# Three transformer layers on one core: bias added on the vector engine, lone matmuls at nine groups, a finer start and two interleaved output blocks

## The reference

```python
# first block: x = x + rms(mixer_a(rms(x))); x = x + (p @ w_pp) * sigmoid(x @ w_pg)
q, k, v, g = split(h @ w_in_a, 4)                # 16 heads of 128
z = q k^T * scale; later = reverse cumulative sum of log_sigmoid(-z), strictly causal
o = exp(log_sigmoid(z) + later) v;  out = (o * silu(g)) @ w_out_a
# second block: the same frame, mixer_b: latent attention
ckv, k_rope = rms(x) @ w_dkv; cq, g = rms(x) @ w_in_b
o = softmax((q_nope k_nope + q_rope k_rope) * scale, chunk mask) v
# third block
q, k, v, gate_b, gate_c, hc = split(rms(x) @ w_in_2)
logits = q1 k1 + rel_bias[bucket(i - j)], the same for q2 k2;   # 8 heads, halves of 64 rows
a = (softmax1 - lam * softmax2) v, rms-normed by head
c = rms(gate_b * causal_conv3(gate_c * hc))
x = x + rms(concat(a, c) @ w_out_2)
x = x + rms((silu(rms(x) @ w_gate) * (rms(x) @ w_up)) @ w_down)   # width 5632
```

## Time and profile before

| | us |
|---|---|
| median of 3 runs (lowest, highest) | 2254.36 (2251.59, 2256.01) |
| the profiled execution | 2259.11 |
| its span, first to last instruction | 2257.3 |
| PE busy | 2207.5 |
| DVE, ACT busy | 1382.3, 1156.2 |

### The profile page before, as it was taken

One profiled execution on the slowest core, in us unless ns is written; L12 is line 12 of the kernel. 1 busy time (PEld: TensorE's weight loads), 2 busy tenths in 40 slices (PEclk: granted clock), 3 DMA queues, 4 the chain that ended last, 5 costly groups with the idle time before them and its releaser, 6 DMA issues.

```text
span 2257.3 us, 29264 instructions
## 1 busy us (share of the span) xinstructions
PE 2207.5 (98%) x12060; PEld 1884.6 (83%) x12060; DVE 1382.3 (61%) x1740; ACT 1156.2 (51%) x1510; POOL 8.9 (0%) x20
## 2 busy tenths in 40 slices
PE   7999999999999999999999999989999999999997
PEld 6888888888878888888887888878888888888886
DVE  6555545557777565577657686567556544565644
ACT  5455454555665555566544443556444444444543
POOL 0000000000000000000000000000000000000000
PEclk9999999999999999999999999999999999999999
DMA  6555555465556445565654545645656666666654
GB/s 218 170 166 162 185 163 181 145 193 187 180 159 182 136 128 162 177 187 178 197 166 142 157 150 163 190 142 177 193 180 196 192 194 193 188 186 196 202 179 151
DMA packets 228677, 394.57 MB, mean 175 GB/s; under 512 B 24921, under 2 KB 50146, under 8 KB 228416
## 3 DMA queue, kind: packets, MB, share of 16 engines
q1 hardware_dynamic: 227312, 389.40, 56.3%
q0 software_dynamic: 800, 2.45, 0.4%
q10 hardware_dynamic: 432, 0.85, 0.1%
HBM read 390.55 MB, written 2.11 MB: 174 GB/s over the span
## 4 chain that ended last, share of the span: by engine, by line
PE 77%; DVE 11%; DMA 6%; ACT 4%; issue 1%; SPq 0%; DVEq 0%; ACTq 0%
PE ps L790 77%; DVE WL L1253 4%; DMA RAW<-in_w_ple_gate 2%; ACT WH L1015 1%; DVE TMP L1253 1%; DVE xT L1253 1%; PE ps L794 1%; DMA RAW<-in_w_out_a 1%; DMA RAW<-in_w_out 1%; ACT T L1015 1%; ACT SQ L1015 1%; DVE T L1253 1%; DMA RAW<-in_w_dkv 1%; DVE ACC L1253 0%; DVE H L1256 0%
## 5 line engine op out<-in xcount | busy, mean ns | idle before, releaser
L1253 DVE TENSOR_TENSOR WL<-RAW,WH 128x1024 fp32r<-128x1024 f32 x734 | 890.1, 1222 | 495.7 <-ACT WH L1015 492.1
L1015 ACT ACTIVATE WH<-RAW 128x1024 fp32r<-128x1024 f32 x734 | 773.1, 1058 | 761.5 <-PE ps L790 316.1
L790 PE MATMUL ps<-H,WH 128*128 128x512 f32 x3152 | 1123.8, 400 | 10.1 <-DVE H L1256 4.8
L790 PE MATMUL ps<-H,WL 128*128 128x256 f32 x3152 | 884.8, 281 | 0.0
L790 PEld LDWEIGHTS ps<-H,WH 128*128 128x128 f32 x3152 | 593.8, 188 | 152.6 <-issue 5.7
L790 PEld LDWEIGHTS ps<-H,WL 128*128 128x128 f32 x3152 | 597.5, 190 | 1.3
L790 PE MATMUL ps<-O,WH 128*128 128x512 f32 x1344 | 477.7, 400 | 7.8 <-DVE WL L1253 3.2
L790 PE MATMUL ps<-O,WL 128*128 128x256 f32 x1344 | 376.1, 280 | 0.0
L790 PEld LDWEIGHTS ps<-O,WH 128*128 128x128 f32 x1344 | 252.7, 188 | 72.6 <-DVE WL L1253 6.3
L790 PEld LDWEIGHTS ps<-O,WL 128*128 128x128 f32 x1344 | 253.9, 189 | 0.3
L790 PE MATMUL ps<-WH,ACTS 128*128 128x512 f32 x704 | 218.3, 390 | 0.0
(11 more groups left out here) (206 smaller groups left out, 1381.2 us busy)
## 6 DMA issues: line engine op xcount, KB each, us to landing
RAW<-in_w_in_a SPq DMA_DIRECT2D x128, 512.0 KB, 4.0
RAW<-in_w_in SPq DMA_DIRECT2D x96, 512.0 KB, 3.9
RAW<-in_w_gate SPq DMA_DIRECT2D x88, 512.0 KB, 4.4
RAW<-in_w_up SPq DMA_DIRECT2D x88, 512.0 KB, 4.5
RAW<-in_w_down SPq DMA_DIRECT2D x88, 512.0 KB, 4.8
RAW<-in_w_ple_gate SPq DMA_DIRECT2D x64, 512.0 KB, 4.5
RAW<-in_w_in_b SPq DMA_DIRECT2D x40, 512.0 KB, 3.8
RAW<-in_w_out_a SPq DMA_DIRECT2D x32, 512.0 KB, 4.1
```

Source lines behind the costliest of these rows:

```text
L790: return e.matmul(o, l, r, start=start, stop=True, skip_group_check=True)
L1015: return e.activation(o, i, f, **kw)
L1253: return e.tensor_tensor(o, x, y, op)
```

## The change

- **Start.** x comes in five pieces (256, 256 and three of 512 KB); the first two chunks hold one k each; pieces 4 and 5 are loaded behind the first `split_lo` steps; the x copies from the third on are ACT's; constants and masks are issued by POOL once the last x piece is in, ahead of its own small loads.
- **Bias.** `c_scores` drops the flips. q is stored with its positions backwards in each half, `c_bias`, a new step, adds RT to the scores in PSUM on DVE, and the product is read backwards by ACT, which takes over the copy and the square. A head's task is two half-chunks longer.
- **Lone matmuls.** A group with `lead` begins with one, in its own bank: block 1 of each output projection, pg0 and pg2 of both blocks, fg1 and fg6.
- **Order.** Taps of `cfir` are steps of their own; the products of the last convolution block are foreground steps; its ones matmul goes to bank 7, so that no two banks of the ring are skipped; the third projection has blocks of 4, 2, 4, 4, 2, its first two fed by turns for the first eight k; masks come first in `a_cum` and `b_scores`; ACT's copy of the latent is a step after DVE's; pp2 and pp3 exchange their second banks.

```diff
+OUTB2 = ((0, 4), (4, 2), (6, 4), (10, 4), (14, 2))
+XPARTS = ((0, 2), (2, 4), (4, 8), (8, 12), (12, 16))
...
-        ci = len(g.chunks) * g.per
-        ks = g.kts[ci:ci + g.per]
+        ci = g.fed
+        ks = g.kts[ci:ci + (1 if ci < g.ones else g.per)]
+        g.fed += len(ks)
...
+        def backwards(ap):
+            dims = [list(d) for d in ap.ap]
+            step, n = dims[-1]
+            return bass.AP(ap.tensor, ap.offset + step * (n - 1), dims[:-1] + [[-step, n]])
...
+                    elif n_ == 0:
+                        pl.begin(g)
+                        pl.begin(gs[1])
+                        for _ in range(2):
+                            pl.feed(g)
+                            pl.feed(g)
+                            pl.feed(gs[1])
+                    if norm == "mixpost" and n_ < 2:
+                        pl.rest(g)
...
-                pl.evict(pp(2, late[0:2]))
+                pl.evict(pp(2, late[0::3]))
                 units[2]()
-                pl.evict(pp(3, late[2:4]))
+                pl.evict(pp(3, late[1:3]))
...
-                units += [both(do("lat_norm", name, 0), do("lat_norm", name, 2)), low[0], low[1]]
+                units += [both(do("lat_norm", name, 0), do("lat_norm", name, 2)),
+                          both(do("lat_high", name, 0), do("lat_high", name, 2)), low[0], low[1]]
...
-                    do("c_scores", hd, bank=[6, 7]), do("c_soft", hd), None, do("c_prob", hd), None, None,
+                    do("c_scores", hd, bank=[6, 7]), do("c_bias", hd), do("c_soft", hd), None, do("c_prob", hd), None, None, None,
...
-                pl.fg.append(task(do("cfir", m, 0), do("cfir", m, 1, makes=[("cfir", m, 1)])))
+                pl.fg.append(task(do("cfir", m, 0, 0), do("cfir", m, 0, 1), both(do("cfir", m, 0, 2), do("cfir", m, 1, 0)),
+                                  do("cfir", m, 1, 1), do("cfir", m, 1, 2, makes=[("cfir", m, 1)])))
...
-                else:
-                    pl.put("conv", m, 0)
-                    pl.put("conv", m, 1)
             pl.h2_read = pl.last_chunk()
-            b = pl.take(2)[0]
-            pl.fg.append(task(None, both(*rstd("conv", b=b)),
+            pl.fg.append(task(do("conv", 1, 0), do("conv", 1, 1, makes=[("conv", 1, 1)]), both(*rstd("conv", b=7)),
...
+                    if first and g.lead and j == 0 and t == 0:
+                        mm(ps[:, b, 0:S], C["ones"], C["cos"], True)
...
-                        mm(ps[:, b, 0:P], q[:, 0:P], k[:, 0:P], True)
-                        mm(ps[:, b, P:384], q[:, P:S], k)
-                        mm(ps[:, b, 0:P], C["flip"], RT[:, hd, P:S])
-                        m = mm(ps[:, b, P:384], C["flip"], RT[:, hd, :])
+                        mm(ps[:, b, 0:P], q[:, P:S], k[:, 0:P], True)
+                        m = mm(ps[:, b, P:384], q[:, 0:P], k)
...
+                elif kind == "c_pv":
+                    pv_ = backwards(halves(ps[:, 6, 0:S]))
+                    ac.wait_ge(at("pv", "C", hd))
+                    act(halves(F2[:, 0, 0:S]), pv_, ACT.Square).then_inc(*ev(act_att, ("csq", hd)))
+                    act(halves(F2[:, 1, 0:S]), pv_, ACT.Copy).then_inc(*ev(act_att, ("ccopy", hd)))
...
+                elif kind == "c_bias":
+                    dv.wait_ge(at("scores", "C", hd), at("in", "rt"))
+                    tt(ps[:, 6:8, 0:P], ps[:, 6:8, 0:P], bc(RT[:, hd, P:S]), ALU.add)
+                    tt(ps[:, 6:8, P:384], ps[:, 6:8, P:384], bc(RT[:, hd, :]), ALU.add).then_inc(*ev(dve_att))
```

More of the change, by code:

```diff
@@ L107 @@
     one: bool = False
+    back: bool = False
+    lead: bool = False
     slow: bool = False
     late: bool = False
+    ones: int = 0
     k0: int = 0
     war: tuple = ()
+    fed: int = 0
     banks: list = field(default_factory=list)
@@ L209, in rest @@
     def rest(self, g):
-        while len(g.chunks) * g.per < len(g.kts):
+        while g.fed < len(g.kts):
             self.feed(g)
@@ L334, in bc, with halves, goal, blocks_of @@
             return ap.unsqueeze(1).broadcast_to([P, n, ap.shape[-1]])
+        def backwards(ap):
+            dims = [list(d) for d in ap.ap]
+            step, n = dims[-1]
+            return bass.AP(ap.tensor, ap.offset + step * (n - 1), dims[:-1] + [[-step, n]])
+        def halves(ap):
+            return ap.rearrange("p (b n) -> p b n", b=2)
+        def goal(g, p):
+            if g.tmp:
+                return TMPG[g.tmp0 + p][:, :, :]
+            dst = g.dst[:, 2 * p:2 * p + g.width(p), :]
+            return backwards(dst) if g.back else dst
+        def blocks_of(norm):
+            return OUTB2 if norm == "mixpost" else OUTB
         def tiles(t, c):
@@ L391, in ordered @@
             xgain(0)()
+            pl.splits(1)
+            xgain(2)()
             xfetch(4)()
-            xgain(2)()
             units = [both(xfetch(c + 2), xgain(c)) if c + 2 < KD else xgain(c) for c in range(4, KD, 2)]
@@ L433, in ordered @@
                 norm = "pre0" if j else ""
-                head(f"q{j}", 512 * j, qT[s], war, scale=P ** -0.5, norm=norm, late=not j)
+                head(f"q{j}", 512 * j, qT[s], war, scale=P ** -0.5, norm=norm, late=not j,
+                     ones=0 if j else 2)
                 head(f"k{j}", D + 512 * j, kT[s], war, norm=norm, late=not j)
@@ L766, in sq_source @@
                 out_ = {"post0": "out0_", "post1": "out1_", "mixpost": "out2_"}[norm]
-                return tiles(T, 2 * i), ("sum", f"{out_}{i // 2}", i % 2) if i < 6 else ("sum", f"{out_}{i - 3}", 0)
+                n_, t0 = next((n_, t0) for n_, (t0, nt) in enumerate(blocks_of(norm)) if t0 <= 2 * i < t0 + nt)
+                return tiles(T, 2 * i), ("sum", f"{out_}{n_}", i - t0 // 2)
             if norm == "kv":
@@ L866, in tensor_engine @@
                     b = 4 + c // 2 % 2
-                    pe.wait_ge(at("in", f"x{c // 4}"), at(*war) if war else None)
+                    part = next(m for m, (c0, c1) in enumerate(XPARTS) if c0 <= c < c1)
+                    pe.wait_ge(at("in", f"x{part}"), at(*war) if war else None)
                     for j in range(2):
@@ L886, in tensor_engine @@
                         mm(ps[:, b, 0:S], C["ones"], SQ[:, 1, :]).then_inc(*ev(summed_sq, ("ones", norm)))
-                elif kind == "lone":
-                    pe.wait_ge(at(*args[0]))
-                    mm(ps[:, 7, 0:S], C["ones"], C["cos"], True).then_inc(*ev(summed_sq, ("lone",)))
                 elif kind == "rcols":
@@ L1066, in scalar_engine @@
                     m.then_inc(*ev(copied, ("free", g.name, 0), ("ready", g.name, 0)))
+                elif kind == "xfetch" and args[0] >= 4:
+                    c = args[0]
+                    ac.wait_ge(at("xt", c))
+                    act(tiles(xT, c), ps[:, 4 + c // 2 % 2, :].rearrange("p (j s) -> p j s", j=2), ACT.Copy).then_inc(
+                        *ev(x_high, ("xcopy", c)))
                 elif kind == "xgain":
@@ L1672, in sync_engine, with load_x @@
             e.dma_start(CS[:, 0:P], cst[:, 0:P]).then_inc(*ev(landed["ident"], ("in", "ident"), by=16))
[L1673 to L1674 removed]
+            def load_x(m):
+                c0, c1 = XPARTS[m]
+                e.dma_start(XN[:, :, P * c0:P * c1], xr[:, :, P * c0:P * c1]).then_inc(
                     *ev(landed[f"x{m}"], ("in", f"x{m}"), by=16))
[L1676 to L1677 removed]
+            for m in range(NRAW):
+                load_x(m)
+                load_chunk(m)
             for kind, *args in steps:
```

102 lines of the change are left out of this document (47 added, 55 removed).

## The result

The changed kernel takes **2224.48 us** (median of four runs, 2222.07 to 2226.67) where the kernel before takes 2254.33. The ratio is 0.9869 with a 95% interval of 0.9853 to 0.9884, so 29.9 us less. Measured again later, beside other kernels, the ratio was 0.9874 (0.9854 to 0.9893). Forecast: 2226 us.

The account below looks back on a forecast made before the run. TensorE was taken to bound the kernel. Start -6.0, bias -13.6, stalls -5.0, lone matmuls -3.2 and the rest -0.5 sum to -28.3 us: 2230.8 us for the profiled execution, 2226 us for the median, range 2215 to 2240.

Parts of the forecast that it names:

- What bounds the kernel: Whole kernel: TensorE, busy 2207.5 of 2257.3 us; gains only by less work, closer spacing, or less of its 50 idle us.
- Part 1: Start: x in pieces, one-k chunks, later constants bring the first dense matmul from 15.74 to 9.3 us; -6.0 us.
- no new wait: Start: chunks 3 and 4 are requested while earlier pairs still lie ahead of TensorE, so no added wait was expected.
- The slow beginning: Start: the first seven pairs, 4.65 us at the 1.2 GHz level, were taken to move along unchanged with the earlier start.
- Part 2: Third block's head scores: without flips, two q-by-k blocks take 1.6 us instead of 3.3; -13.6 us for eight heads.
- rival A: Head scores: the two 64-row blocks overlap, saving 0.65 us more per head, 5.2 us more; 2221 us; chance 0.12.
- Part 3: Convolution and third projection: reordering answers stalls of 1.51, 1.10, 0.40, 0.38 and 2.36 us, sum 5.75; -5.0 us.
- no stall above 0.5 us: Sign to check: TensorE has no longer stall between 1140 and 1400 us of the new span.
- Part 4: Eight more lone matmuls at group starts cost 3.4 us and buy 6.6 through 6.3 ns closer pair spacing; -3.2 us.
- Rival B: Convolution stalls only move and close spacing does not last: -0.5 and +2 instead of -8.2; 2236 us; chance 0.22.
- C: Start gains nothing, as ACT with the x copies becomes the bound or the slow level lasts longer; 2232 us; chance 0.06.
- D: Third block's heads: DVE, adding the bias in PSUM, becomes the bound and takes back the gain; 2256 us; chance 0.03.

Follow-up runs that it names:

- experiment 12: Changed kernel with the old start: x in four pieces, whole chunks, x copies on DVE, constants and masks from ACT's queue at once; 2229.01 us, ratio 0.9877.
- experiment 1: Changed kernel with the two 64-row score blocks of each third-block head half a chunk apart, dense pairs between them; 2231.46 us, ratio 0.9879.
- experiment 2: Changed kernel with the second block's scores reordered: masks, then both 64-row rope products side by side, then the 128-row products; 2218.21 us, ratio 0.9820.
- experiment 4: Kernel before, flips kept, with the third block's two 64-row score products side by side, then the two flips; 2250.69 us, ratio 0.9961.
- experiment 7: Changed kernel with the convolution and the third projection's block order as they were before; 2232.12 us, ratio 0.9891.
- experiment 6: Changed kernel without the eight new lone matmuls, the one at fg6 kept; 2227.80 us, ratio 0.9877.
- experiment 3: Changed kernel with no weight split put ahead of the first group's last chunk, so q0's eviction comes before the next split; 2222.68 us, ratio 0.9840.
- experiment 11: Changed kernel with rope products side by side, q0's eviction ahead of split and square, lone matmul at fg2 instead of fg1, none at fg6; 2221.10 us, ratio 0.9851.
- experiment 8: Changed kernel with the second block's rope products side by side and q0's eviction ahead of the next split and square; 2216.72 us, ratio 0.9826.
- experiment 10: Changed kernel with rope products side by side, q0's eviction ahead of split and square, and fg1's lone matmul moved to fg2; 2217.31 us, ratio 0.9832.
- experiment 5: The changed kernel itself measured once more, unedited; 2227.57 us, ratio 0.9874 to the kernel before.
- experiment 9: Changed kernel with the lone matmul of group fg1 moved to fg2; 2225.50 us, ratio 0.9875.

## Why the prediction was right, and where its steps were not

The time was hit within 2 us, but in part by luck: of the five terms the start and the lone matmuls brought less than was counted and the flips more, and the errors nearly cancel.

**What bounds the kernel** held: TensorE's busy share is 98% still, and the gain came by the three ways named.

**Part 1, the start: mis-sized.** The step said 6.0 us, with the first dense matmul at 9.3 and "no new wait". It came at 10.42, since the third piece of x was awaited until 9.65, where the forecast had it in at 7.8 and its transposes done at 8.9. The step that failed is the sentence on the wait: TensorE, 5.3 us ahead, overtakes the weight transfers and the evictions that stand behind a split waiting for one. About 2.2 us are left at the 161st pair (experiment 12) and 0.7 to 1.8 in the time. The slow beginning did not move along unchanged: the full clock is granted from 12.9 us, 2.5 us behind the first dense matmul, before from 20.8, 5.1 us behind it. This too differs from run to run: 3.2 to 5.2 us in the other traces with the new start, 3.8 and 4.8 in the other two with the old one.

**Part 2, the flips: the forecast's price wrong, rival A's right.** The forecast took two blocks in a row (1.6 us, -13.6) and gave rival A, that they overlap, 0.12. The step that failed is the price of the second block, 0.65 us, which costs nothing. Experiments 1, 2 and 4 show the overlap three times: two 64-row blocks on different rows and banks take 0.86 us where one takes 0.85. The gain is 8 x 2.26 = 18.1 us. (The forecast set 1.6 against 3.3 us, where its own rows have 3.12 from start to dense work; on that measure 0.86 came out, where its sign said 1.6 and rival A 1.0.) The price of a change between 64 and 128 rows, 0.2 us, fits: in the rope step of experiment 2, one hidden block (0.65) and two changes (0.4) make 1.05, and 1.04 was measured. No run measures a change by itself. The rule of the Trainium skill, TensorEngine Tiling (Array Packing), Tiling Modes, that different tiles run in parallel, agrees with these traces, for fp32 operands of 64 rows and 128 columns. The argument against it in the prediction (each fp32 matmul is two passes) did not hold: eight such passes side by side take as long as four. On DVE and ACT the sizes were right. In the heads the two adds in PSUM are 0.43 and 0.69 us, q's backward eviction 0.588 beside 0.586 for k's, and DVE is at 75% (76 forecast).

**Part 3, the stalls: right in size, with one moved.** The forecast was -5.0. The stall at 1187 us is gone (1.51). Of the four around the projection (4.24) 0.56 is left:

```profile
1381.38 0.67 PE L828 MATMUL ps<-ACC,CS 128*128 128x256 f32 x2 [0.56 <-DVE ACC L1299]
```
Together 5.2 us; undoing the convolution's part costs 4.6 (experiment 7). The sign "no stall above 0.5 us" failed all the same: this one has 0.56, and the one at 1311 us has 0.71, where waits of 0.31 and 0.52 stood nearby before. Another thing was not forecast. The half clock that begins shortly behind the wait for the last sum of squares, and spans the layer's last wait (4.8 us in both), lasts 6.8 us now and lasted 10.2. Before, and after:

```profile
1498.80:1508.90 10.10, 5.29 (x17) 4.23 (x16) 8.72 (x18) 4.45 (x9) 0.00 (x0) 0.50 0.06 18
```

```profile
1467.00:1473.70 6.70, 3.08 (x9) 2.67 (x10) 6.43 (x13) 2.75 (x5) 0.00 (x0) 0.50 0.00 0
```
Half of TensorE's busy time in it is lost to the clock: 2.6 us before, 1.5 now. It varies, though, 6.8 and 10.2 us in the two traces of the same changed kernel, and 6.8 in experiment 4, a form of the kernel before, so that this 1 us is a matter of the run and not of the change.

**Part 4, the lone matmuls: a gain in some runs only.** The cost, 0.43 each, held. The step said that at fg1 the 0.43 us of delay would outlast the stall at 1558 us, and the spacing stay close: in the first trace it did not, by 0.03 us in one matmul, and the 4.0 us counted for groups 1 to 5 did not come; in six of the eight traces with a lone matmul at fg1 they did. The third projection is close in the first trace and was wide before (175 of 192 pairs), but it is close without the lone matmul as well (experiment 6) and wide in three traces with it, so that the step's share there is not shown. Over all the time shows 0.2 us where -3.2 was forecast, with more than that as its uncertainty, and the two traces say +1.4 and -3.1. The step that failed is the one that took the close spacing for a property of the program. Rival B had this half right for some runs, "the close spacing does not last", and the other half, that stalls only move, wrong but for the 0.71 us.

**Rivals C and D** did not decide. No wait of TensorE on ACT's copies of x shows, though the start gave so little that the time alone does not exclude C's number. DVE, with the bias, holds up TensorE once, in the chain that ends at 1311 us, for 0.71 us; D needed 3.5 us in every head.

**Sum.** For forecast against measured: start 6.0, some 2; flips 13.6, 18.1; stalls 5.0, 5.2; lone matmuls 3.2, between -1.4 and 3.1, about 0 in the time; that makes some 25 of the 29.9 us. The other 4 to 5 us are where the forecast had 0.5. TensorE's waits from the heads to group fg1 fell by 6.5 us in all, 1.3 more than those 5.2; of this 0.8 is the wait for the last sum of squares (2.13 before, 1.34 now). The close spacing of the third projection is worth about 1 us in this trace. The 1.9 us between pairs 161 and 2817 and the run's own share (the half clock, about 1) are the rest, and no run here separates them.

**A better version.** With the order of experiment 2 the ratio is 0.9820, 0.9826 and 0.9832 in three kernels, and 0.9851 in the one without the lone matmul at fg6, where the changed kernel has 0.9869 and 0.9874. That is about 10 us under the changed kernel by ratio (10.9 and 8.2 for experiments 8 and 10 beside their neighbours 5 and 9), and 37 to 41 under the kernel before for the first three.

## What to carry to other kernels

Products that use half of the rows belong side by side, on different rows and, as here, different banks, with no product on all rows between them: the same matmuls in another order were worth 8 us twice. Work that starts earlier only helps as far as the next queue reaches, so look what the engine overtakes (here, an eviction behind a split that waits for its transfer). And an edit worth a few microseconds must be judged from several executions where a state that lasts hundreds of matmuls hangs on one being 0.03 us late.

## What the runs showed of the hardware that was not expected

- Two fp32 products of 64 rows, each of 128 and 256 columns, take 0.85 us alone and 0.86 us side by side.
- After one TensorE matmul that is 0.03 us late, 512- and 256-column fp32r pairs run at 0.3533 us instead of 0.3467, for as many as 623 pairs. A lone fp32 matmul was followed by the close spacing in many places but not in all: in the third projection of experiments 1, 3 and 11, and behind most scores of the heads, fp32 too, the pairs are wide.
- The granted clock fell to half for 3.4 us (once 6.8, experiment 8) at stalls of TensorE of 1.76 to 3.25 us, in some executions and not in others: at the stall near 641 us in eleven traces of fourteen, and not behind 3.08 us in experiment 2. Behind the new stall at 41 us it fell in experiments 1 and 7 (waits of 1.86 and 1.76 us) and not in the changed kernel (2.36 and 2.01).
